# Staging the rows of w_out through the halves of x_res in the first block of a pool and mLSTM layer

## The reference

```
h    = rms_norm(x) * (1 + scale(c)) + shift(c)
proj = h @ w_in                       # u, z_pool, q, k, v, o, z_mlstm, gates
pool = (trailing means of u - u) @ w_pool * ls * silu(z_pool)      # 4 groups of 128
q, k = silu(causal depthwise conv of 4 taps)
hm   = mLSTM over chunks of 128 positions (4 heads), normalised, * sigmoid(o) * silu(z)
out  = rms_norm(x + gate(c) * (concat[pool, hm] @ w_out))
```

## Time and profile before

| | |
|---|---|
| median of 3 runs | 1937.85 us (1936.37 to 1939.13) |
| profiled execution | 1939.13 us |
| its span | 1937.3 us |
| TensorE matmuls busy | 1850.4 us, 96% |
| VectorE busy | 1085.5 us, 56% |
| ScalarE busy | 470.5 us, 24% |
| GpSimd busy | 235.3 us, 12% |
| DMA queue of SyncE | 322.00 MB, 48.1% of 16 engines' span |
| w_out loads | 8 of 512 KB, median 5.4 us from issue to landing |
| writes to w_kept from the ring | 48 of 512 KB, median 5.6 us |
| loads of units of w_in | 48 of 256 KB, median 4.3 us |

### The profile page before, as it was taken

One profiled execution on the slowest core, in us unless ns is written; L12 is line 12 of the kernel. 1 busy time (PEld: TensorE's weight loads), 2 busy tenths in 40 slices (PEclk: granted clock), 3 DMA queues, 4 the chain that ended last, 5 costly groups with the idle time before them and its releaser, 6 DMA issues.

```text
span 1937.3 us, 25856 instructions
## 1 busy us (share of the span) xinstructions
PE 1850.4 (96%) x8897; PEld 1526.4 (79%) x8897; DVE 1085.5 (56%) x2429; ACT 470.5 (24%) x971; POOL 235.3 (12%) x214
## 2 busy tenths in 40 slices
PE   2798999999999999999999999999999999999998
PEld 1577878888878887788877888788877888778886
DVE  7777575535746276562755437553573627645273
ACT  1234432212221223121222122221222212222221
POOL 0433213000120002100020000300012000210000
PEclk9999999999999999999999999999999999999999
DMA  9589942555235642455424553255514564245421
GB/s 293 180 261 305 310 161 82 191 195 196 77 134 193 210 161 87 142 195 207 142 77 173 191 207 104 88 200 193 194 66 148 190 212 155 79 153 194 174 98 65
DMA packets 123193, 323.76 MB, mean 167 GB/s; under 512 B 11612, under 2 KB 49204, under 8 KB 123060
## 3 DMA queue, kind: packets, MB, share of 16 engines
q1 hardware_dynamic: 123060, 322.00, 48.1%
HBM read 275.82 MB, written 46.14 MB: 166 GB/s over the span
## 4 chain that ended last, share of the span: by engine, by line
issue 53%; PE 20%; DVE 12%; DMA 7%; POOL 2%; ACT 1%; SPq 1%; DVEq 0%; POOLq 0%; ACTq 0%
PE ps_acc L452 5%; PE ps_acc L453 5%; PE ps_acc L454 5%; DMA w_kept<-sb_w_split 2%; DMA sb_x_in<-x 2%; DVE sb_dmat L1048 2%; DVE sb_k_w L1048 1%; DVE sb_x_res L1472 1%; DMA sb_x_res<-x 1%; POOL sb_h_rs L954 1%; DVE sb_x_res L1485 1%; DMA out<-sb_x_res 1%; DMA sb_w_raw<-w_in 1%; DVE sb_x_in L1030 1%; DVE sb_mixm_lo L1385 1%
## 5 line engine op out<-in xcount | busy, mean ns | idle before, releaser
L452 PE MATMUL ps_acc<-sb_hT_hi,sb_w_split 128*128 128x512 f32 x1536 | 601.3, 391 | 1.0 <-POOL sb_w_split L942 1.0
L453 PE MATMUL ps_acc<-sb_hT_lo,sb_w_split 128*128 128x512 f32 x1536 | 599.5, 390 | 0.0
L454 PE MATMUL ps_acc<-sb_hT_hi,sb_w_split 128*128 128x512 f32 x1536 | 599.3, 390 | 0.0
L454 PEld LDWEIGHTS ps_acc<-sb_hT_hi,sb_w_split 128*128 128x128 f32 x1536 | 289.0, 188 | 60.7
L452 PEld LDWEIGHTS ps_acc<-sb_hT_hi,sb_w_split 128*128 128x128 f32 x1536 | 289.4, 188 | 60.1 <-POOL sb_w_split L942 1.9
L453 PEld LDWEIGHTS ps_acc<-sb_hT_lo,sb_w_split 128*128 128x128 f32 x1536 | 289.1, 188 | 59.7
L954 POOL TENSOR_TENSOR sb_h_rs<-sb_h_var,sb_mhalf 128x4 f32<-128x4 f32 x32 | 32.4, 1012 | 1143.0 <-DVE sb_h_var L1351 1143.0
L1272 DVE SCALAR_TENSOR_TENSOR sb_acc_cv<-sb_shifted,sb_par,sb_acc_cv 128x512 f32<-128x512 f32 x192 | 146.2, 761 | 6.8
L452 PE MATMUL ps_acc<-sb_wo_hi,sb_mixm_hi 128*128 128x512 f32 x256 | 104.9, 410 | 0.0
L1295 DVE TENSOR_TENSOR sb_oz<-sb_tanh,sb_oz 128x512 f32<-128x512 f32 x32 | 22.1, 692 | 146.6 <-ACT sb_tanh L843 146.6
L454 PE MATMUL ps_acc<-sb_wo_hi,sb_mixp_lo 128*128 128x512 f32 x256 | 101.2, 395 | 0.0
(11 more groups left out here) (214 smaller groups left out, 2764.3 us busy)
## 6 DMA issues: line engine op xcount, KB each, us to landing
sb_w_split<-w_kept SPq DMA_DIRECT2D x400, 512.0 KB, 3.2
w_kept<-sb_w_split SPq DMA_DIRECT2D x48, 512.0 KB, 5.6
sb_x_res<-x SPq DMA_DIRECT2D x34, 512.0 KB, 4.6
out<-sb_x_res SPq DMA_DIRECT2D x32, 512.0 KB, 2.6
sb_x_in<-x SPq DMA_DIRECT2D x30, 512.0 KB, 5.4
sb_w_raw<-w_in SPq DMA_DIRECT2D x48, 256.0 KB, 4.3
sb_qT<-w_ada SPq DMA_DIRECT2D x4, 1024.0 KB, 6.4
sb_kT<-w_ada SPq DMA_DIRECT2D x4, 1024.0 KB, 5.4
```

The lines of the kernel that those rows point to most:

```text
L452: pe.matmul(dst, st_hi, mv_hi, start=start, stop=False)
L453: pe.matmul(dst, st_hi, mv_lo, start=False, stop=False)
L454: return pe.matmul(dst, st_lo, mv_hi, start=False, stop=stop)
```

## The change

wo_raw is no longer there. The rows of w_out are loaded into the two halves of x_res by turns, row k into half k % 2, scaled there, and split from there into wo_hi and into a wo_lo with a place of its own. Rows 0 and 1 are loaded in the setup, behind the last w_ada load and a wait for the transposes of x. Row k from 2 on is loaded at unit 24+2k, in place of 12+2k, and SyncE waits before it until `wout_low(k-2)` is done. The load of the residual at unit 50 of the first block waits for the last `wout_low`. The instructions on VectorE and ScalarE keep their number, shapes and places.

```diff
-    wo_at, _ = nc.bump_sbuf(KT * D * 4)
...
-        wo_hi = sb("wo_hi", [P, KT, D], F32R)
-        wo_raw = nc.alloc_sbuf_tensor_at("sb_wo_raw", [P, KT, D], F32, offset=wo_at)
-        wo_lo = nc.alloc_sbuf_tensor_at("sb_wo_lo", [P, KT, D], F32R, offset=wo_at)
+        wo_hi, wo_lo = sb("wo_hi", [P, KT, D], F32R), sb("wo_lo", [P, KT, D], F32R)
...
-        wout_loaded = [sem(f"wout_loaded{k}") for k in range(KT)]
+        wout_loaded = [sem(f"wout_loaded{i}") for i in range(2)]
...
             def load_wout(k):
-                sp.dma_start(wo_raw[:, k, :], w_out[0, P * k:P * k + P, :]).then_inc(wout_loaded[k], 16)
+                if k >= 2:
+                    sp.wait_ge(wout_lo_done, k - 1)
+                sp.dma_start(x_res[:, k % 2, :], w_out[0, P * k:P * k + P, :]).then_inc(wout_loaded[k % 2], 16)
...
             load_ada(11)
+            sp.wait_ge(x_T, PREPS)
+            load_wout(0)
+            load_wout(1)
             sp.dma_start(fg[:, :], final_g.partition_broadcast(P)).then_inc(fg_loaded, 16)
...
-                wout_units = {V_UNITS + 2 * k + 4: k for k in range(KT)} if first else {}
+                wout_units = {V_UNITS + 2 * (WOUT_TILE + k) + 4: k for k in range(2, KT)} if first else {}
...
                     if m == 50:
+                        if first:
+                            sp.wait_ge(wout_lo_done, KT)
                         load_res(b, 0)
                         load_res(b, 1)
...
             def wout_high(k):
                 act.wait_ge(wout_scaled, k + 1)
-                act.activation(wo_hi[:, k, :], wo_raw[:, k, :], ACT.Copy).then_inc(wout_hi_done, 1)
+                act.activation(wo_hi[:, k, :], x_res[:, k % 2, :], ACT.Copy).then_inc(wout_hi_done, 1)
...
-                dve.wait_ge(wout_loaded[k], 16)
+                dve.wait_ge(wout_loaded[k % 2], 16 * (k // 2 + 1))
                 for n in range(2):
                     s = slice(512 * n, 512 * n + 512)
-                    last = V.tensor_tensor(wo_raw[:, k, s], wo_raw[:, k, s], kv[n][:, :], ALU.mult)
+                    last = V.tensor_tensor(x_res[:, k % 2, s], x_res[:, k % 2, s], kv[n][:, :], ALU.mult)
...
-                V.tensor_tensor(wo_lo[:, k, :], wo_raw[:, k, :], wo_hi[:, k, :].bitcast(F32),
+                V.tensor_tensor(wo_lo[:, k, :], x_res[:, k % 2, :], wo_hi[:, k, :].bitcast(F32),
                                 ALU.subtract).then_inc(wout_lo_done, 1)
```

## The result

| | before | after |
|---|---|---|
| median | 1937.11 us (4 runs, 1936.02 to 1939.13) | 1954.74 us (4 runs, 1953.99 to 1955.04) |
| profiled execution, its span | 1939.13 us, 1937.3 us | 1954.56 us, 1952.7 us |
| last fold product starts | 215.11 us | 230.17 us |

The ratio is 1.0088, with an interval of 1.0075 to 1.0100: slower, by about 17 us where the forecast was 8.6. From the last fold product to the end of the span it is 1722.2 us before and 1722.5 after, so the loss lies ahead of that product.

The account below looks back on a forecast made before the run. TensorE was taken to bound the kernel, with all changes falling in the first block. A 10.1 us gain against 18.7 us of rounds gave +8.6 us on 1937.85, so 1946.4 us; range of 8 in 10, 1935 to 1953.

Parts of the forecast that it names:

- the relief: Tiles 1 to 8: w_out loads leave SyncE's queue, so TensorE's waits of 1.0 and 5.23 us go.
- The closed round: From tile 8: SyncE's wait, odd unit's load, split, wout_high and wout_low feed the next wait; 9.3 us against TensorE's 6.88.
- The steps behind it: After wout_low(6): fold_product(6) starts 2.1 us later, behind mixm_lo, and fold_product(7) 6.88 us after that, at 223.7.
- The front: Setup: two 512 KB loads at about 70 us delay writes to w_kept by up to 3.7 us; costed at nothing.
- Rival 1: Odd units 29 to 39 land below about 3.65 us, so the kernel gets faster: 1933.5, down to 1927.7; chance 0.12.
- Rival 3: Repeated TensorE waits in the fold tiles keep the clock low: +27 us, 1965; chance 0.04.
- The 4.14 us from copy to tanh: Tile 7: time from ScalarE's copy out of PSUM to tanh, taken from 129.84 and 133.98, towards wout_low(0) ending at 158.9.
- The cover: First block: 10.1 us gain if nothing else stood in the way, last fold product at 205.0 instead of 215.11.
- the slow tile: Tile 8: takes 2.5 us more than needed at granted clock 0.68 behind the dmat wait; taken as gone.
- The likeliest case's own range: Forecast total with the odd unit's landing at its bounds: +2.9 to +18.6 us, 1940.7 to 1956.4.

Follow-up runs that it names:

- two edits at two of its links: Changed kernel with SyncE's wait and w_out load moved behind the odd unit: 1946.79 us, 1.0039; or with ScalarE's wout_high ahead of the odd unit's split: 1948.84 us, 1.0049.
- The cut of the taps: Changed kernel with two conv taps cut to 16 of 512 columns in the first block, work left out: 1947.94 us, ratio 1.0044.
- the run with ScalarE's copies: Changed kernel with low parts of units 10 to 23 plainly copied by ScalarE, GpSimd's subtraction left out: 1949.45 us, ratio 1.0051.
- the late loads without the wait: Kernel before, eight w_out places kept, rows 0 and 1 loaded in setup, 2 to 7 at units 28 to 38, no wout_low wait: 1943.51 us, ratio 1.0022.

## Why the prediction was right in sign and short in size

**Right.** What bounds the kernel before, and that the relief takes the waits of tiles 0 to 8: no wait for dmat, tile 7 over at 150.5 (forecast 150.9). The closed round: 9.3 us forecast, 9.1 to 9.4 measured in five of six rounds, with the parts as given above; two edits at two of its links each broke it, by SyncE's waits. The steps behind it: the seventh product 2.2 us after wout_low(6) (forecast 2.1), the last 6.88 us on. The front cost nothing that shows at tile 7. Rival 1 fell, since the odd units landed in 5.1 to 5.3 us, and once in 7.4, not under 3.65. Rival 3 fell in its size: the clock was 0.69 and 0.81 in two windows behind waits of 5.8 and 2.6 us and 0.57 over 214 to 220 us behind the wait of 4.43 us, but 0.96 over 180 to 215 us, and the next product started 9.3 us on, as in the other rounds.

**The step that failed.** "Tile 7 ends at 150.9, its copy out of PSUM starts then". It started at 154.71. I took TensorE's pace for the pace of the tile. VectorE takes 6.43 us a conv tile in the kernel after, with GpSimd splitting units beside it. The change made SyncE's round of 7 us a tile an estimated 5.3 us and I put TensorE, with 5.5, next in line; VectorE was. The trace of before had the warning, if not the number. Its VectorE in tiles 5 and 6, between the last operations of tiles 4, 5 and 6 (L1282):

```profile
141.79 1.35 DVE L1282 SCALAR_TENSOR_TENSOR sb_kT<-sb_tanh,sb_acc_cv 128x512 f32<-128x512 f32 x1 [1.93 <-ACT sb_tanh L833]
...
144.45 1.13 DVE L1268 TENSOR_SCALAR sb_acc_cv<-sb_shifted,sb_par 128x512 f32<-128x512 f32 x1 [1.10 <-ACT sb_shifted L828]
...
149.02 0.68 DVE L1282 SCALAR_TENSOR_TENSOR sb_kT<-sb_tanh,sb_acc_cv 128x512 f32<-128x512 f32 x1
...
151.48 1.12 DVE L1268 TENSOR_SCALAR sb_acc_cv<-sb_shifted,sb_par 128x512 f32<-128x512 f32 x1 [1.58 <-ACT sb_shifted L828]
...
156.03 0.68 DVE L1282 SCALAR_TENSOR_TENSOR sb_kT<-sb_tanh,sb_acc_cv 128x512 f32<-128x512 f32 x1
```

Less its wait for the copy out of PSUM, a tile is 7.23 - 1.10 = 6.1 us and 7.01 - 1.58 = 5.4 us: no slack against 5.5. The 4.14 us from copy to tanh that I used had such a stretched operation in it as well. This set the first wout_low back by 163.2 - 158.9 = 4.3 us. The cut of the taps and the run with ScalarE's copies show it.

**A term that was mis-sized.** From the end of wout_low(0) to that of wout_low(6) it was 57.9 us where 55.8 was forecast for the six rounds, all of the difference in the fifth, where the odd unit landed in 7.4 us (201.28 to 208.73). It came in two of three runs of the kernel after, and not with ScalarE's copies. Its cause is open: half the w_out bytes did not take it away, and no other run was aimed at it.

The sum with the two: 223.7 + 4.3 + 2.1 = 230.1, and the last product started at 230.17, 15.1 us later than before. The profiled executions differ by 15.4 us and the medians by 17.6; the other 2 us are of the size by which the runs of before differ (1936.02 to 1939.13), and no stretch shows them.

**The cover.** The 10.1 us of gain were counted against a last product at 205.0. Without any wait it came at 217.4: 4.9 us from VectorE's and ScalarE's lateness at the first product (161.66 against 156.8), and 7.6 us from seven steps of 8.0 in place of 6.88. Of these, 2.5 us are the first step at the lower clock, which I had counted as gained with the wait for dmat ("the slow tile"), and 5.1 us are the queue. That the moved loads would meet the fold pieces in a queue round of 8.25 us was no step and no rival of mine; the earlier trace rows showed 0.98 of DMA share there already. It didn't enter the sum, because the round of 9.3 is longer than that of 8.25 and, as I read it, hides it; it does mean that the wait is to be charged with 12.8 us at the last product, and the late place of the loads with 2.3 us.

**The range.** The likeliest case's own range, 1940.7 to 1956.4, held the time; I cut the stated one at 1953, and 1954.74 lies outside. That the wider one held it was luck: its bounds came from the landing alone, which was forecast right in five of six rounds, while the step that failed had none.

The Trainium skill has the contention: "SBUF — State Buffer", section "Who interferes with whom", says that VectorE and GpSimd share one pair of ports under an exclusive lock, so that one of them stands while the other holds it. The trace agrees in that a copy which takes 0.17 us by itself takes 1.16 and 1.22 us beside GpSimd's subtraction; the ports themselves no run here shows.

## What to carry to other kernels

Where a change takes a bound away, work out the pace of every engine in that stretch, with its operations as long as they are beside the others', before you name the next bound. A wait that is put into an in-order queue is to be followed through what stands behind it until it either leaves the loop or comes back to its own release; if it comes back, the round is a sum of landings and fixed steps. Here moving the wait by one place gave back 0.49%, and halving the bytes of the row 0.2%. And opening one round gives only what the next bound, here SyncE's queue, leaves over. A load moved out of one full stretch of the queue is to be priced where it lands.

## What the runs showed of the hardware

- A VectorE operation beside a GpSimd subtraction of 128 x 512 (1.3 us) takes 0.6 to 1.1 us longer whatever its own size: a copy of 3 columns 1.16 to 1.22 us in place of 0.17, a pass over 512 columns 1.58 in place of 0.53 in the kernel after and 1.13 in that before. Two of them in a tile are the 2 us by which VectorE's tile of 4.4 to 4.5 us becomes 6.43.
- With loads and writes of 256 and 512 KB in one queue at a DMA share of 1.01 and 354 GB/s (the late loads without the wait), a write of 512 KB takes 6.6 to 6.8 us to land; over the whole kernel after its median is 5.0 us.
- In the kernel after the granted clock was 0.50 over 162 to 166 us behind a wait of 5.79 us, 0.72 over 174 to 180 behind one of 2.56 us and 0.57 over 214 to 220 behind one of 4.43 us, and it was 1.00 over 193 to 202 us behind one of 2.11 us.
